# Mixture-of-experts blocks of 32 rows on four column tiles, in place of 64 rows on two

## The chip, the cores and the metric

The kernel runs on one core of a Trainium2 chip. The metric is the device time of one execution in microseconds. All matrix products here are in float32; a 512-column product is recorded as two passes of TensorE, each with its own weight load.

## The reference

Two layers work on 256 context and 1024 latent tokens of width 1024. Layer 0 mixes tokens by attention and a two-way recurrent scan, layer 1 by differential attention. Behind each stands a mixture of experts: every token picks one of four groups and in it two of eight experts, so 32 experts share 2560 assignments in layer 0 and 2048 in layer 1 (context rows are no longer needed there). An expert computes

```python
def run_block(args):
    xblk, e = args
    return (jax.nn.silu(xblk @ w_gate[e]) * (xblk @ w_up[e])) @ w_down[e]
```

with `w_gate[e]` and `w_up[e]` of 1024 x 512 and `w_down[e]` of 512 x 1024. The assignments are sorted by expert and each expert's segment is padded to whole blocks. The block size doesn't enter the result. Each expert has 6.3 MB of weights, each layer 201 MB.

## The kernel before

The program is a chain of phases with a barrier between them. For the mixture of layer `l` they are: `norm_phase` with the tag `nb` (RMSNorm and modulation, rows `h` to DRAM, their transpose kept in SBUF), `route_phase` (router products, choice of experts, ranks, the slot of each assignment, and a small table for the sequencers), `experts_phase`, and `combine_phase` (gathers two result rows a token, weights and adds them).

`experts_phase` (L2175) takes tiles of 128 rows, each two blocks of `BR = 64` rows; the two blocks of a tile may belong to different experts. Layer 0 has 28 tiles, layer 1 has 27 (56 and 53 blocks of 64, from the routing of the reference's inputs). The five engines each run their own loop over the tiles:

- SyncE fetches weights, expert after expert, into a ring of `WR = 3` slots: gate, up and down are one DMA of 2 MB each (L2221). `fetch` waits until the expert that held the slot has done this part (`g_done`, `u_done`, `y_done`); `arrived` (L2224) then passes on that the expert before has landed (`w_ready`, L2227). The view is `"e (k p) n -> p e k n"`: partition p holds rows p, p + 128, ... of the matrix, in pieces of 2 KB for gate and up and 4 KB for down.
- GpSimd gathers the 128 rows of the next tile by token number, 4 KB a row (L2276).
- TensorE multiplies. `products` (L2301) runs one product for the two blocks side by side: output partitions 0 to 63 are block 0 (L2306, weight slot through a register), partitions 64 to 127 block 1 (L2309, slot chosen by three `pe.If`, one for each slot). The order in a tile is gate, up, transposes of the next tile's rows (L2291), transposes of the hidden values (L2321), down in two halves. Every tile reads a code from the table and takes the slots and the number of experts needed from it (L2297 to L2299).
- ScalarE copies the transposed rows, applies SiLU to the gate bank, copies half of the result and issues its store to `yb` (L2354).
- VectorE multiplies SiLU(gate) by up (L2367), copies the transposed hidden values (L2369) and the other half of the result (L2373).

In layer 0 SyncE also writes zeros to the tiles of `yb` that no block fills (L2245). Within `route_phase` VectorE works out the table (L2135 to L2170) while GpSimd scatters the token numbers to their slots.

Of the kernel before, what the change touches and what calls it, by code (L numbers as in the profile page):

```python
# [21 lines left out]
P = 128  # L22
# [20 lines left out]
MODS = 6 * D  # L43
SHIFT1, SCALE1, GATE1, SHIFT2, SCALE2, GATE2 = range(6)
# [115 lines left out]
def norm_phase(nc, sems, tag, d, layer, which, src, hT, ident_dram, rows_out=None, first=0):  # L160
# [5 lines left out]
    with ExitStack() as ctx:  # L166
# [19 lines left out]
        lead_done = s.sem("lead_done")  # L186

# [13 lines left out]
        with nc.Block() as block:  # L201
# [61 lines left out]
            def _(dve):  # L263
# [7 lines left out]
                def body(j, n, par, cond):  # L271
                    for u in range(2):
# [12 lines left out]
                        nc.vector.tensor_tensor(h[:, u, :], h0[:, u, :], mod[:, cond, 0, :], ALU.add).then_inc(h_done, 1)  # L285
# [8 lines left out]
            @block.tensor  # L294
            def _(pe):
                pe.sem_inc(tr_free, 4)
                pe.wait_ge(const_in, 16 * 5)

                def body(j, n, par, cond):
                    for u in range(2):  # L300
                        pe.wait_ge(h_done, 2 * n + u + 1)
                        for b in range(2):

                            pe.wait_ge(tr_free, 4 * n + 2 * u + b + 1)
                            for k in range(4):
                                kk = 4 * b + k
                                last = nc.tensor.transpose(tr[u][b][:, k * P:(k + 1) * P], h[:, u, kk * P:(kk + 1) * P], ident[:, :])
                            last.then_inc(tr_done, 1)
                pairs(pe, body)
# [1626 lines left out]
BR = 64  # L1936
NPM = (2 * TOK + NE * (BR - 1)) // BR // 2 + 1
NPT = NPM + 1
NBT = 2 * NPT
WR = 3  # L1940
CAP = TOK // BR


T_NP, T_EXP, T_PEND, T_CODE = 0, 1, 1 + NE, 1 + 2 * NE
T_COLS = T_CODE + NPT

# [13 lines left out]
def route_phase(nc, sems, tag, d, layer, hT, first, slot_dram, slots, gates, tok, table):  # L1960
# [3 lines left out]
    with ExitStack() as ctx:  # L1964
# [21 lines left out]
        cmp = s.sb("cmp", [P, NBT * NE])  # L1986
        sf = s.sb("sf", [P, 2, T])
        tf = s.sb("tf", [P, T_COLS])
        bo = s.sb("bo", [P, 2, NBT])
        back = s.sb("back", [NPT, P])  # L1990
# [7 lines left out]
        NC_IN = 16 * 8  # L1998

        with nc.Block() as block:  # L2000
            @block.sync
            def _(sp):
                wv = lambda w: w.rearrange("(k p) n -> p k n", p=P)
# [9 lines left out]
                sp.dma_start(desc[:, :], d["desc"]).then_inc(c_in, 16)  # L2013

                sp.wait_ge(zeroed, 1)
                sp.dma_start(slot_dram.rearrange("(n p) o -> n (p o)", p=P), zero[0:NPT, :]).then_inc(filled, 16)
                sp.wait_ge(scattered, 16 * 2 * T)
                sp.dma_start(back[:, :], slot_dram.rearrange("(n p) o -> n (p o)", p=P)).then_inc(back_in, 16)
# [14 lines left out]
            def _(pe):  # L2033
# [15 lines left out]
                pe.wait_ge(back_in, 16)  # L2049
                nc.tensor.transpose(bankT[:, 0:NPT], back[:, :], ident[0:NPT, 0:NPT]).then_inc(back_t, 1)  # L2050

# [11 lines left out]
            def _(dve):  # L2063
# [71 lines left out]
                c.did(V.tensor_scalar(steps[:, 0:2 * NPT], iota[:, 0:2 * NPT], float(BR), None, ALU.mult))  # L2135
# [18 lines left out]

                c.did(V.tensor_scalar(steps[:, 0:NPM], iota[:, 0:NPM], 2.0, None, ALU.mult))
                tally(tf[:, T_PEND:T_PEND + NE], rows_(col(BO), NE, NPM), cols_(steps[:, 0:NPM], NE, NPM), ALU.is_gt, NE, NPM)
                c.did(V.tensor_copy(tf[:, T_NP:T_NP + 1], tf[:, T_PEND + NE - 1:T_PEND + NE]))
# [4 lines left out]
                c.did(V.tensor_scalar(steps[:, 0:NE // WR + 1], iota[:, 1:NE // WR + 2], float(WR), None, ALU.mult))  # L2162
                q = NE // WR + 1
                tally(bo[:, 1, :], rows_(bo[:, 0, :], NBT, q), cols_(steps[:, 0:q], NBT, q), ALU.is_ge, NBT, q)
                c.did(V.scalar_tensor_tensor(out=bo[:, 1, :], in0=bo[:, 1, :], scalar=-float(WR), in1=bo[:, 0, :], op0=ALU.mult, op1=ALU.add))
                code = tf[:, T_CODE:T_CODE + NPT]
                c.did(V.tensor_scalar(code, bo[:, 0, 1:NBT:2], float(WR * WR), float(WR * WR), ALU.mult, ALU.add))
                c.did(V.scalar_tensor_tensor(out=code, in0=bo[:, 1, 0:NBT:2], scalar=float(WR), in1=code, op0=ALU.mult, op1=ALU.add))
                c.did(V.tensor_tensor(code, bo[:, 1, 1:NBT:2], code, ALU.add))
                c.did(V.tensor_copy(table[:, :], tf[0:1, :]))  # L2170
                dve.wait_ge(back_t, 1)
                c.did(V.tensor_copy(tok[:, :], bankT[:, 0:NPT]))


def experts_phase(nc, sems, tag, d, layer, rows, yb, tok, table, fill):  # L2175
# [7 lines left out]
    HT = EH // P  # L2183
    with ExitStack() as ctx:
# [3 lines left out]
        idx = s.sb("idx", [P, 1], U32)  # L2188
        x = s.sb("x", [P, D])
        xT = s.sb("xT", [P, KT, P])  # L2190
        sg, a = s.sb("sg", [P, EH]), s.sb("a", [P, EH])
        aT = s.sb("aT", [P, HT, P])
        y = s.sb("y", [P, D])
        tr = [s.ps(f"tr{b}") for b in range(2)]
        bG, bU, bA = s.ps("bG"), s.ps("bU"), s.ps("bA")
        bY = [s.ps(f"bY{b}") for b in range(2)]
        c_in, idx_done, x_in, xtr, xT_done = (s.sem(n) for n in (
            "c_in", "idx_done", "x_in", "xtr", "xT_done"))
        w_in = [[s.sem(f"w_in{part}{u}") for u in range(WR)] for part in ("gate", "up", "down")]
        w_ready = [s.sem(f"w_ready_{part}") for part in ("gate", "up", "down")]  # L2200
        g_done, u_done, sg_done, a_done, atr, aT_done, y_done, ye_act, ye_dve, y_out = (s.sem(n) for n in (
            "g_done", "u_done", "sg_done", "a_done", "atr", "aT_done", "y_done", "ye_act", "ye_dve", "y_out"))
        go, ended, filled, zeroed = (s.sem(n) for n in ("go", "ended", "filled", "zeroed"))
        zero = s.sb("zero", [P, D])
        wv = lambda name: d[name][layer].rearrange("e (k p) n -> p e k n", p=P)

        def load(eng, col, most, least=0):
            return eng.value_load(table[0:1, col], min_val=least, max_val=most)

        with nc.Block() as block:  # L2210
            @block.sync
            def _(sp):
                sp.dma_start(ident[:, :], d["ident"]).then_inc(c_in, 16)

                def fetch(u, e, tiles, part):

                    if tiles is not None:

                        sp.wait_ge((g_done, u_done, y_done)[part], (1, 1, 2)[part] * tiles)
                    name, at, kk, n = (("moe_w_gate", 0, KT, EH), ("moe_w_up", UP, KT, EH), ("moe_w_down", DOWN, HT, D))[part]  # L2220
                    sp.dma_start(w[:, u * WCOLS + at:u * WCOLS + at + kk * n].rearrange("p (o k n) -> p o k n", o=1, n=n),  # L2221
                                 wv(name)[:, ds(e, 1), :, :]).then_inc(w_in[part][u], 16)
# [6 lines left out]
                def step(o, u, free, before):  # L2229

                    e = load(sp, ds(o + T_EXP, 1), NE - 1)
                    tiles = load(sp, ds(o + (T_PEND - WR), 1), NPM, 1) if free else None
# [7 lines left out]
                if fill:  # L2240

                    sp.wait_ge(zeroed, 1)
                    n = load(sp, slice(T_NP, T_NP + 1), NPM)
                    with sp.Fori(n, NPT) as i:
                        sp.dma_start(yb[ds(i * P, P), :], zero[:, :]).then_inc(filled, 16)  # L2245
# [8 lines left out]
                if fill:  # L2254
# [3 lines left out]
                    sp.wait_ge(filled, 16 * NPT)  # L2258
                    sp.sem_inc(ended, 1)

            @block.gpsimd
            def _(pool):
                nc.gpsimd.memset(zero[:, :], 0.0).then_inc(zeroed, 1)
                n = load(pool, slice(T_NP, T_NP + 1), NPM)
                nc.gpsimd.tensor_copy(idx[:, :], tok[:, 0:1]).then_inc(idx_done, 1)
                pool.wait_ge(idx_done, 1)
                nc.gpsimd.indirect_dma_start(x[:, :], None, rows[:, :], bass.IndirectOffsetOnAxis(idx[:, 0:1], 0)).then_inc(x_in, 16)
                with pool.Fori(0, n) as i:

                    pool.wait_ge(x_in, 16 * i + 16)  # L2270
                    nc.gpsimd.tensor_copy(idx[:, :], tok[:, ds(i + 1, 1)]).then_inc(idx_done, 1)
                    pool.wait_ge(idx_done, i + 2)
                    pool.wait_ge(xtr, 2 * i + 2)

                    pool.sem_inc(go, 1)
                    nc.gpsimd.indirect_dma_start(x[:, :], None, rows[:, :], bass.IndirectOffsetOnAxis(idx[:, 0:1], 0)).then_inc(x_in, 16)  # L2276
# [352 lines left out]
```

## Time and profile before

| | us |
|---|---|
| median of 3 runs | 5791.07 |
| lowest, highest | 5783.55, 5791.42 |
| the profiled execution | 5788.05 |
| its span | 5785.7 |

The profile is one execution taken by the hardware profiler. The span runs from its first to its last instruction. "PE" is TensorE's matmuls, "PEld" its weight loads, which overlap them, "PEldq" its sequencer's own work (loads of registers, arithmetic, branches), which isn't counted as busy. PEclk is the granted clock of TensorE as a share of 2.4 GHz. "DMA share" is the mean busy share of the 16 DMA engines; overlapping packets let it pass 1.

### The profile page before, as it was taken

What the parts mean: (1) busy time and instruction counts of PE and PEld (TensorE: products, weight loads), DVE (VectorE), ACT (ScalarE), POOL (GpSimd) and SP (SyncE); (2) the same over time, 40 slices, a digit from 0 to 9 for tenths busy, and PEclk for the clock granted to TensorE, in tenths of its full rate; (3) what the DMA queues carried; (4) which work ended last, traced back from release to release, by engine and by line L of the source; (5) the groups of instructions that cost most, each with busy time, mean ns of one, the idle gap of its engine ahead of it and who ended that gap; (6) DMA issues with size and microseconds to landing.
All of it is one profiled execution on the core that took longest, in us unless ns stands there. A gap on an engine that the chain in (4) does not pass through costs nothing. (4 is left out here: it accounts for less than half of the span.)

```text
span 5785.7 us, 71070 instructions
## 1 busy us (share of the span) xinstructions
PE 4182.2 (72%) x23474; PEld 2739.1 (47%) x23475; DVE 2196.7 (38%) x4254; ACT 1422.0 (25%) x3188; POOL 639.3 (11%) x1135
## 2 busy tenths in 40 slices
PE   5597599395876949574499983598199955497893
PEld 1385377284765838453133321487056644132331
DVE  0312544666556656624000002411677733200003
ACT  0210254343333424212011110210056622011111
POOL 0000000131322313300100002000300010100001
PEclk9798799697988969786799996799599977799997
DMA  9421100101010010133886697322510023799943
GB/s 336 147 86 68 62 9 9 38 1 25 10 25 10 0 34 1 46 128 109 312 339 235 228 377 282 118 89 76 193 49 10 11 98 105 274 364 397 374 165 145
DMA packets 350063, 778.83 MB, mean 135 GB/s; under 512 B 52000, under 2 KB 95284, under 8 KB 349796
## 3 DMA queue, kind: packets, MB, share of 16 engines
q1 hardware_dynamic: 297640, 624.64, 30.1%
q10 hardware_dynamic: 37696, 103.04, 4.6%
q0 software_dynamic: 14544, 48.79, 2.4%
q8 instruction: 105, 1.72, 0.1%
q14 instruction: 78, 0.64, 0.0%
HBM read 656.45 MB, written 122.58 MB: 135 GB/s over the span
## 5 line engine op out<-in xcount | busy, mean ns | idle before, releaser
L2306 PE MATMUL ex_bG<-ex_w,ex_xT 128*64 x880 | 424.7, 639 | 134.5 <-SPq L2227 77.3
L2306 PE MATMUL ex_bY<-ex_w,ex_aT 128*64 x880 | 392.6, 599 | 74.5 <-DVE ex_aT L2369 59.7
L2309 PE MATMUL ex_bG<-ex_w,ex_xT 128*64 128x512 f32 x880 | 424.7, 639 | 0.0
L367 PE MATMUL p_acc<-hT,p_wh 128*128 128x512 f32 (+1 forms) x1056 | 376.2, 356 | 24.6 <-DVE p_wl L379 24.6
L2309 PE MATMUL ex_bY<-ex_w,ex_aT 128*64 128x512 f32 x880 | 392.8, 600 | 0.0
L2306 PE MATMUL ex_bU<-ex_w,ex_xT 128*64 x880 | 386.6, 592 | 0.0
L2309 PE MATMUL ex_bU<-ex_w,ex_xT 128*64 128x512 f32 x880 | 386.6, 592 | 0.0
L2367 DVE TENSOR_TENSOR ex_a<-ex_sg,ex_bU 128x512 f32<-128x512 f32 x55 | 37.9, 688 | 917.9 <-PE ex_bU L2309 917.9
L367 PE MATMUL p_acc<-hT_rest,p_wh 128*128 128x512 f32 (+1 forms) x1056 | 375.7, 356 | 0.0
L367 PE MATMUL p_acc<-hT,p_wl 128*128 128x512 f32 (+1 forms) x1056 | 375.2, 355 | 0.0
L2306 PEld LDWEIGHTS ex_bG<-ex_w,ex_xT 128*64 128x64 f32 x880 | 127.9, 148 | 415.3 <-issue 415.3
L703 PE MATMUL ad_S<-ad_K,ad_q 64*128 64x512 f32 (+1 forms) x768 | 193.5, 584 | 125.2 <-DMA ad_lqk<-in_od_lk 120.8
L2306 PEld LDWEIGHTS ex_bY<-ex_w,ex_aT 128*64 128x64 f32 x880 | 116.7, 138 | 306.5 <-issue 306.5
L777 DVE TENSOR_SCALAR_CACHE_REDUCE ad_p<-ad_S 128x512 f32<-128x512 f32 (+1 forms) x384 | 215.7, 600 | 100.5 <-PE ad_S L703 100.5
L2306 PEld LDWEIGHTS ex_bU<-ex_w,ex_xT 128*64 128x64 f32 x880 | 120.6, 137 | 248.7 <-issue 248.7
L388 DVE COPY p_o<-p_acc 128x512 f32<-128x512 f32 x88 | 49.1, 558 | 469.5 <-PE p_acc L367 468.7
L367 PEld LDWEIGHTS p_acc<-hT,p_wh 128*128 128x128 f32 x1056 | 200.9, 190 | 53.9 <-issue 25.4
L1354 PE MATMUL rs_bankZ<-rs_X,rs_Bm 128*128 128x128 f32 x1280 | 224.7, 277 | 0.0
L1351 PE MATMUL rs_bankY<-rs_ident,rs_X 128*128 128x128 f32 x640 | 185.1, 289 | 47.3 <-DVE rs_Bm L1558 39.0
L367 PEld LDWEIGHTS p_acc<-hT_rest,p_wh 128*128 128x128 f32 x1056 | 201.0, 190 | 27.9
L367 PEld LDWEIGHTS p_acc<-hT,p_wl 128*128 128x128 f32 x1056 | 200.6, 190 | 28.2
L1450 ACT ACTIVATE rs_Y<-rs_bankY 128x256 f32<-128x256 f32 x320 | 122.4, 384 | 350.3 <-PE rs_bankZ L1354 350.2
(362 smaller groups left out, 8841.4 us busy)
## 6 DMA issues: line engine op xcount, KB each, us to landing
ex_w<-in_moe_w_gate SPq DMA_DIRECT2D x64, 2048.0 KB, 17.8
ex_w<-in_moe_w_up SPq DMA_DIRECT2D x64, 2048.0 KB, 21.2
ex_w<-in_moe_w_down SPq DMA_DIRECT2D x64, 2048.0 KB, 18.1
mods_w<-in_mod_w SPq DMA_DIRECT2D x24, 2048.0 KB, 13.0
projT_dram<-p_o ACTq DMA_DIRECT2D x44, 640.0 KB, 2.9
yb_dram<-ex_y ACTq DMA_DIRECT2D x55, 512.0 KB, 6.3
p_w<-in_od_w_in SPq DMA_DIRECT2D x12, 1024.0 KB, 5.1
n_x<-x_dram SPq DMA_DIRECT2D x20, 512.0 KB, 4.1
```

Source lines behind the costliest of these rows:

```text
L367: mm = nc.tensor.matmul(acc[u % 2][c][:, 0:n], a[:, u // 2, k, at], b[:, k, t0:t0 + n], start=k == 0 and x == 0, stop=k == KT - 1 and x == 2)
L388: nc.vector.tensor_copy(o[:, u % 2, t0:t0 + n], acc[u % 2][c][:, 0:n]).then_inc(dve_ev, 1)
L703: x = nc.tensor.matmul(S[j % 2][c][:, 0:w], q[h, pair, t * P - q_from:(t + 1) * P - q_from], K[h, kmap(pair), a:a + w], start=True, stop=True)
L777: nc.vector.tensor_scalar(p[:, u, c, a:a + w], S[j % 2][c][:, 0:w], 1.0, None, ALU.mult, ALU.max, accum_out=top[:, u, c, i:i + 1]).then_in ...
L1351: nc.tensor.transpose(bankY[g][:, dr * P:(dr + 1) * P], X[:, g, dr, :], ident[:, :])
L1354: x = nc.tensor.matmul(to, Bm[:, g, dr, l, :], X[:, g, dr, :], start=True, stop=True)
L1450: aa.did(f"X{g}" if l == 1 else f"Y{l}{g}", nc.scalar.activation(to[:, g, :, :], bankY[g][:, 0:256].rearrange("p (d t) -> p d t", d=2), AC ...
L2306: nc.tensor.matmul(bank[0:BR, :], stationary[:, k, 0:BR], w[:, ds(slot0 + (offset + k * n), 512)], start=k == 0, stop=k == tiles - 1)
L2309: m = nc.tensor.matmul(bank[BR:P, :], stationary[:, k, BR:P], w[:, at:at + 512], start=k == 0, stop=k == tiles - 1)
L2367: nc.vector.tensor_tensor(a[:, :], sg[:, :], bU[:, :], ALU.mult).then_inc(a_done, 1)
```

## The change

- **Blocks.** `BR` is 32. A block is the unit of every loop. There are 97 in layer 0 and 83 in layer 1 (from the same routing); before, with the padding, there were 28 x 4 = 112 and 27 x 4 = 108 such units of 32 rows.
- **Four column tiles.** One matmul call fills 32 output partitions and takes 256 columns of weights. In `hidden` the four groups are the left and right half of gate and the left and right half of up, into one bank `bH`: partitions 0 to 63 gate, 64 to 127 up. In `down` the four groups are the quarters of the 1024 output columns, in one bank `bY`.
- **Rows as quarters.** `h` in DRAM is cut into four pieces of 256 values a row; one gather fetches 32 rows x 4 pieces of 1 KB to 128 partitions. The token list is spread to quarters in `route_phase`.
- **Neighbouring weight rows on a partition.** The gate and up views are `(p k)`: partition p holds rows 8p to 8p + 7, 16 KB in one piece. Down is `(g p h)` with h = 2: pieces of 8 KB. To match, the norm phase writes `h` in another order of columns (`placed`), its transposes read with a step of 2, and so do the transposes of the experts phase.
- **Order on TensorE.** A block's `down` is put behind the next block's `hidden`. Tiles x, xT, sg, a, aT, y and all PSUM banks are doubled.
- **Evictions.** ScalarE keeps SiLU and the stores, VectorE makes all PSUM copies.
- Each block reads the table twice (`place`), once for `hidden` and once for `down`, and each has a chain of three `pe.If`.

```diff
-BR = 64
+BR = 32
+CAP = TOK // BR
+NBM = (2 * TOK + NE * (BR - 1)) // BR
+NBT = NBM + 3
 WR = 3
...
-                        nc.vector.tensor_tensor(h[:, u, :], h0[:, u, :], mod[:, cond, 0, :], ALU.add).then_inc(h_done, 1)
+                        nc.vector.tensor_tensor(placed(h[:, u, :]), natural(h0[:, u, :]), natural(mod[:, cond, 0, :]), ALU.add).then_inc(h_done, 1)
...
-                        sp.wait_ge((g_done, u_done, y_done)[part], (1, 1, 2)[part] * tiles)
+                        sp.wait_ge((h_done, h_done, y_done)[part], tiles)
...
+                    if part < 2:
+                        sp.dma_start(to.rearrange("p (o k n) -> p o k n", o=1, n=n),
+                                     d[name][layer].rearrange("e (p k) n -> p e k n", k=kk)[:, ds(e, 1), :, :]).then_inc(w_in[part][u], 16)
+                    else:
+                        sp.dma_start(to.rearrange("p (o g n) -> p o g n", o=1, g=2),
+                                     d[name][layer].rearrange("e (g p h) n -> p e g (h n)", g=2, h=2)[:, ds(e, 1), :, :]).then_inc(w_in[part][u], 16)
...
+                def turn_rows(p, landed, b=None):
+                    pe.wait_ge(x_in[p], 16 * landed)
+                    if b is not None:
+                        pe.wait_ge(a_done, b + 1)
+                    for e in range(2):
+                        t = nc.tensor.transpose(bX[p][:, e * P:(e + 1) * P], x[:, p, e:XC:2], ident[:, :])
+                    t.then_inc(xtr, 1)
+                def place(b):
+                    code = load(pe, ds(b + T_CODE, 1), WR * (NE + 1) - 1, WR)
+                    return code // WR, code % WR
+                def hidden(p, u):
+                    for c in range(XG):
+                        for e in range(2):
+                            for g in range(4):
+                                at = u * WCOLS + (0, UP)[g // 2] + (2 * c + e) * EH + g % 2 * HC
+                                m = nc.tensor.matmul(bH[p][g * BR:(g + 1) * BR, 0:HC], xT[:, p, e, c, :], w[:, at:at + HC],
+                                                     start=c == 0 and e == 0, stop=c == XG - 1 and e == 1)
+                    m.then_inc(h_done, 1)
+                def down(p, u):
+                    for k in range(HT):
+                        for g in range(4):
+                            at = u * WCOLS + DOWN + k * D + g * XC
+                            m = nc.tensor.matmul(bY[p][g * BR:(g + 1) * BR, 0:XC], aT[:, p, k % 2, k // 2, :], w[:, at:at + XC], start=k == 0, stop=k == HT - 1)
+                    m.then_inc(y_done, 1)
+                def turn_hidden(p):
+                    for h in range(2):
+                        t = nc.tensor.transpose(bA[p][:, h * 2 * BR:(h + 1) * 2 * BR], a[2 * BR:P, p, h:HC:2], ident[2 * BR:P, 2 * BR:P])
+                    t.then_inc(atr, 1)
+                def block_down(b, p):
+                    need, slot = place(b)
+                    pe.wait_ge(w_ready[2], need)
+                    pe.wait_ge(aT_done, b + 1)
+                    for u in range(WR):
+                        with pe.If(slot == u):
+                            down(p, u)
...
                 with pe.Fori(0, n) as i:
+                    for q in PAR:
+                        b, p = 2 * i + q + 1, 1 - q
+                        need, slot = place(b)
+                        for part in range(2):
+                            pe.wait_ge(w_ready[part], need)
+                        pe.wait_ge(xT_done, b + 1)
                         for u in range(WR):
+                            with pe.If(slot == u):
+                                hidden(p, u)
+                        block_down(b - 1, 1 - p)
+                        turn_rows(p, i + q + 2, b)
+                        turn_hidden(p)
```

## Rows read from the trace of the kernel before

**Rows 1.** The page's first part: busy time, share of the span, instructions.

```profile
PE 4182.2 (72%) x23474; PEld 2739.1 (47%) x23475; DVE 2196.7 (38%) x4254; ACT 1422.0 (25%) x3188; POOL 639.3 (11%) x1135
```

**Rows 2.** Windows over both expert phases: stretch, length, busy us, PEclk, DMA share, GB/s.

```profile
2777.00:3537.00 760.00, 649.68 (x3024) 235.91 (x3026) 57.29 (x83) 100.95 (x142) 33.32 (x59) 0.94 0.83 310
4960.00:5700.00 740.00, 624.71 (x2924) 228.59 (x2924) 55.26 (x80) 97.40 (x137) 31.94 (x55) 0.94 0.83 310
```

**Rows 3.** Timeline of TensorE in one tile: start, us, engine, line, operation, [idle before].

```profile
5443.11 0.59 PE L2306 MATMUL ex_bU<-ex_w,ex_xT 128*64 x1
...
5449.55 0.59 PE L2306 MATMUL ex_bU<-ex_w,ex_xT 128*64 x1
...
5450.08 1.10 PE L2291 MATMUL ex_tr<-ex_ident,ex_x 128*128 128x128 f32 x8
5451.02 0.65 PE L2321 MATMUL ex_bA<-ex_ident,ex_a 128*128 128x128 f32 x4
5453.03 0.64 PE L2306 MATMUL ex_bY<-ex_w,ex_aT 128*64 x1 [1.36 <-DVE ex_aT L2369]
...
5466.81 0.59 PE L2306 MATMUL ex_bU<-ex_w,ex_xT 128*64 x1
```

**Rows 4.** Waits of TensorE in the two expert phases: total us, times, longest.

```profile
PE ex_bG L2306 <- SPq L2227: 27.1, 4, 8.4
PE ex_bY L2306 <- DVE ex_aT L2369: 24.5, 20, 1.7
...
PE ex_bG L2306 <- SPq L2227: 50.3, 6, 19.6
```

**Rows 5.** Windows: experts bound by weights; 2 KB pieces of mod_w; 5 KB pieces.

```profile
5300.00:5420.00 120.00, 89.76 (x390) 31.06 (x392) 6.96 (x11) 12.68 (x18) 4.23 (x8) 0.87 1.04 397
60.00:140.00 80.00, 57.32 (x222) 10.30 (x218) 8.77 (x13) 0.00 (x0) 0.00 (x0) 0.85 0.95 356
4190.00:4200.00 10.00, 8.94 (x24) 3.45 (x24) 6.19 (x24) 3.00 (x5) 0.00 (x0) 0.50 1.03 419
```

**Rows 6.** TensorE's sequencer by line: count, ns min/median/max, first and last start.

```profile
L2304 PEldq COMPARE_BRANCH  x660: 68/200/379, 2788.5 to 5695.9; - x165
...
L2208 PEldq TENSOR_LOAD <-table x57: 297/304/492, 2778.0 to 5673.0; - x57
L2208 PEldq FUSED_REGOPS  x57: 151/157/165, 2778.5 to 5673.3; - x57
...
L2295 PEldq FUSED_REGOPS  x55: 59/59/64, 2785.8 to 5672.9; - x55
```

**Rows 7.** Sequencer's branches at 5443.2 to 5449.9; then matmuls of ex_bU after.

```profile
L2304 PEldq COMPARE_BRANCH  x1: 200/200/200, 5445.7 to 5445.7; - x1
...
5445.75:5450.00 4.25, 4.25 (x22) 1.28 (x18) 0.00 (x0) 1.00 1.02 396
```

**Rows 8.** Sequencer before and in the first product of ex_bY; then ten small transposes.

```profile
L2304 PEldq COMPARE_BRANCH  x2: 68/138/207, 5452.4 to 5452.7; - x2
...
L2306 PEldq FUSED_REGOPS  x4: 46/46/150, 5452.8 to 5453.3; - x4
...
2713.83 0.78 PE L2042 MATMUL rt_bankL<-rt_ident,rt_lgT 36*128 36x36 f32 x10 [0.56 <-ACT rt_lgT L2056]
```

**Rows 9.** Evictions of PSUM (page, timeline), and landing of the row gathers.

```profile
L2367 DVE TENSOR_TENSOR ex_a<-ex_sg,ex_bU 128x512 f32<-128x512 f32 x55 | 37.9, 688 | 917.9 <-PE ex_bU L2309 917.9
...
2713.31 0.38 ACT L2056 ACTIVATE rt_lgT<-rt_acc 36x256 f32<-36x256 f32 x1 [2.86 <-PE rt_acc L2037]
...
DMA to landing us min/median/max: 4.0/7.5/9.0
```

**Rows 10.** VectorE's timeline: norm rows, a stepped read in routing, tok.

```profile
2662.25 1.23 DVE L285 TENSOR_TENSOR nb_h<-nb_h,nb_mod 128x1024 f32<-128x1024 f32 x1 [0.24 <-DMA h_dram<-nb_h]
...
2718.02 0.72 DVE L2093 TENSOR_REDUCE rt_w<-rt_big 128x80 f32<-128x320 f32 x1
...
2774.89 0.20 DVE L2172 CAST tok<-rt_bankT 128x37 uint32<-128x37 f32 x1 [18.12 <-PE rt_bankT L2050]
```

More of the change, by code:

```diff
@@ L2182, in experts_phase @@
     UP, DOWN = KT * EH, 2 * KT * EH
-    HT = EH // P
+    HT, HC = EH // P, EH // 2
+    PAR = range(2)
     with ExitStack() as ctx:
@@ L2263, in _, with gather @@
                 nc.gpsimd.memset(zero[:, :], 0.0).then_inc(zeroed, 1)
[L2264 to L2267, printed above, removed]
-                with pool.Fori(0, n) as i:
[L2270 to L2276, printed above, removed]
+                n = half(pool)
+                def gather(b, p):
+                    nc.gpsimd.tensor_copy(idx[:, p:p + 1], tok[:, ds(b, 1)]).then_inc(idx_done, 1)
+                    pool.wait_ge(idx_done, b + 1)
+                    pool.sem_inc(go, 1)
+                    nc.gpsimd.indirect_dma_start(x[:, p, :], None, pieces, bass.IndirectOffsetOnAxis(idx[:, p:p + 1], 0)).then_inc(x_in[p], 16)
+                gather(0, 0)
+                gather(1, 1)
+                pool.wait_ge(xtr, 1)
+                gather(2, 0)
+                with pool.Fori(0, n) as i:
+                    for u in PAR:
+                        pool.wait_ge(xtr, 2 * i + u + 2)
+                        gather(2 * i + u + 3, 1 - u)
             @block.tensor
@@ L2280, in _ @@
                 pe.wait_ge(c_in, 16)
-                n = load(pe, slice(T_NP, T_NP + 1), NPM)
-                def turn(i, again):
-                    pe.wait_ge(x_in, 16 * i + 16)
-                    for b in range(2):
-                        if again:
-                            pe.wait_ge(xT_done, 2 * i - 1 + b)
-                        for k in range(4):
-                            t = nc.tensor.transpose(tr[b][:, k * P:(k + 1) * P], x[:, (4 * b + k) * P:(4 * b + k + 1) * P], ident[:, :])
-                        t.then_inc(xtr, 1)
@@ L2356, in _, with gated, store @@
-                act.wait_ge(y_out, 16 * n + 16)
+                n = half(act)
+                def gated(b, p):
+                    act.wait_ge(h_done, b + 1)
+                    nc.scalar.activation(sg[2 * BR:P, p, :], bH[p][0:2 * BR, 0:HC], ACT.Silu).then_inc(sg_done, 1)
+                def store(b, p):
+                    act.wait_ge(ye_done, b + 1)
+                    act.dma_start(yb[ds(b * BR, BR), :].rearrange("t (c n) -> c t n", c=XG), y[:, p, :]).then_inc(y_out[p], 16)
+                for u in PAR:
+                    act.sem_inc(y_out[u], 16)
@@ L2485, in _ @@
                     act.wait_ge(x_out[u], 16 * rounds)
-CONSTS = ("cos", "sin", "ident", "ones", "blockones", "headones", "headcols", "tri", "first", "levels", "before", "iota", "tokid", "desc")
+CONSTS = ("cos", "sin", "ident", "ones", "blockones", "headones", "headcols", "tri", "first", "levels", "before", "iota", "tokid", "desc", "quad")
 def build(nc, d, out):
```

213 lines of the change are left out of this document (106 added, 107 removed).

## The prediction

> **What bounds the kernel now.** I read the page first. TensorE is busy for 4182 of 5786 us, more than any other engine [rows 1]. The change touches the two expert phases, so I cut windows over them: 760 us and 740 us, together 1500 us, with TensorE busy for some 85% and the DMA engines for 83% [rows 2]. Neither is full over the phase, so the limit must change from tile to tile. The timeline of a tile gives the first side. In the product of up, 15 passes lie between 5443.11 and 5449.55, 0.429 us each; a pass is 512 columns on both column tiles at once. From one tile's up to the next tile's it is 23.7 us [rows 3] (23.5 below, as most tiles are a little shorter). The other side is the weights. Where each block brings a new expert, the DMA engines are at 1.04 with 397 GB/s [rows 5]. At that rate an expert's 6.29 MB take 15.8 us and each tile's 1.05 MB of rows and results 2.6 us more: 34.2 us for a tile with two new experts, 18.4 with one. TensorE's waits for weights stand in the list of waits, 27 and 50 us, on ten tiles [rows 4].
>
> Both together explain the phases. Layer 0 has 9 tiles of 28 with two new experts, layer 1 has 11 of 27 (from the routing of the reference's inputs). The sum over tiles of the larger side is 19 x 23.5 + 9 x 34.2 = 754 us and 16 x 23.5 + 11 x 34.2 = 752 us: 1506 against 1500 measured. I use the same rule for the changed kernel and take the 6 us off again.
>
> **Array time of a block.** A pass of `hidden` or `down` has 256 columns, so 0.214 us if its four groups run side by side as the two do now. `hidden` has 8 steps of two passes, 3.42 us; `down` has 4, 1.71 us. Twelve transposes took 0.94 us for the first eight, 0.117 each, and 0.10 us passes between the last product and the first of them [rows 3]. Four transposes with two such changes are 0.67 us. The array needs 5.8 us a block. Four blocks make 23.2 us for 128 rows, the same as a tile today; what is saved is padding, 180 blocks in place of 220 units of 32 rows (97 and 83 against 112 and 108). With 5.8 us a block nothing would be lost.
>
> **What the sequencer needs.** Here I find the cost. Today a tile reads the table once and runs 12 tests of an If (660 for 55 tiles); the load takes 0.30 us, the operation behind it 0.16, the address 0.06, a taken branch 0.20 and one not taken 0.07 [rows 6]. Between two such instructions about 0.06 us passes: the first test starts at 5452.4, the second at 5452.7, the registers at 5452.8, the first matmul at 5453.03 [rows 3, 8]. A read of the table with what follows (some three more operations of 0.05 and seven gaps) is then 1.1 us; a chain of three tests is 0.26 + 0.26 + 0.13 = 0.65 us, part of it ahead of the body and part behind.
>
> Today this is hidden by a queue. The last branch of the up product starts at 5445.7, with all its matmuls issued, and 22 matmuls run in the 4.25 us after it, two of which had begun: 20 are queued, ten passes of two [rows 7]. With four matmuls in a pass of 0.214 us the same 20 last for five passes, 1.07 us. The changed block has two reads of the table and two chains. From the last matmul of `hidden` to the first of `down` the sequencer needs 0.65 + 1.1 + 0.1 for a second wait = 1.85 us, 0.8 more than the queue holds; a restart costs 0.05 (0.64 us for the first pass's matmul, 0.59 for others [rows 3]): 0.85 us idle. From the last matmul of `down` it needs the rest of the chain (0.26), two waits (0.2), half a loop end (0.15), the table (1.1), three waits (0.3) and the next chain's head (0.39): 2.4 us, against 1.07 of queue and 0.67 of transposes: 0.7 us idle. The block comes to 5.8 + 0.85 + 0.7 = 7.4 us. The ends: 5.8 if the queue hides all, 8.2 if nothing of `down` is queued when its waits come. I take 7.4, since the rows price each part.
>
> Other waits of a block stay inside these. `down` of block b-1 needs aT, copied during `hidden` of block b. The transposes of b wait for its product: SiLU on 256 columns (0.38 us) and a VectorE product of half of today's 0.69 us, with a drain of 0.2 behind `hidden`, some 1.2 us [rows 9], under idle and `down` (2.6). Gathers land in 7.5 us, at most 9.0, plus 2 us on GpSimd, and have two blocks, 14.8 us. VectorE's four copies are 1.6 us a block. These cost nothing; at 5.8 us a block the gather (11 of 11.6 us) would be late next.
>
> **Weights.** Pieces of 16 KB and 8 KB replace 2 KB and 4 KB. At full DMA share, 2 KB pieces give 356 / 0.95 = 375 GB/s and 5 KB pieces 419 / 1.03 = 407 [rows 5]. On 16 engines that is 87 ns and 201 ns a piece: 13 ns fixed and 37 ns per KB. At 16 KB this gives 433 GB/s, at 8 KB 424, so 14.6 us an expert in place of 15.8. No row shows such pieces; the bounds are 14.6 and 15.8 (no gain), above it if long pieces hold up the short ones. I take 14.6, as both rows lie on the straight line. Rows and results are 0.74 us a block (1 KB pieces by the same line, 128 each way).
>
> **The sum.** An expert of n blocks costs the larger of 7.4 n and 14.6 + 0.74 n. With one or two blocks it is the weights (15.3 and 16.1), from three on TensorE. Layer 0 has 7 experts with one block, 12 with two, and 66 blocks in the rest: 107 + 193 + 488 = 788 us. Layer 1 has 17, 5 and 56 blocks: 260 + 81 + 414 = 755 us. Together 1543, less the same 6, is 1537: 37 us more than now. The expert with 18 blocks alone costs 133 us, today 106.
>
> Small parts: the stepped write of 18 norm tiles, between 0 and 1 us each (today 1.23 us for 1024 elements; a stepped read took 0.72 for 320 [rows 10]), on a path with other waits: 3 us. The table of VectorE grows by 3 us, but VectorE idles for 18 us ahead of `tok` [rows 10]: 0. Two more operations behind it and the wait for up before the first product: 2 us. Total +42: the profiled execution at 5788.05 becomes 5830; the median of the runs shown is 3 us above it (5791), so 5833.
>
> The Trainium skill, TensorE: Matmul & The Clock Gate, the table at its head, gives TensorE a queue of 64 instructions. By this rule 32 loads and 32 matmuls would be queued, 1.7 us; the rows show 20 matmuls [rows 7], and the measurement decides. What the rule would make of the time is the first rival.
>
> **Rivals.** First, the sequencer stays hidden, because the queue holds more or the tests and reads cost less than I add up. It decides below 7.1 us a block, where the sum (768 + 738 - 6) equals today's 1500. For it: today no idle stands between tiles. Against: the count of 20, and 0.64 us from test to matmul. With 6.1 us a block the sum is 703 + 683 - 6 = 1380, so -120 + 5: 5676. Chance 0.25. By the skill's 64 entries the gaps shrink to about 0.2 and 0.1 us, 6.1 us a block.
>
> Second, the pieces gain nothing: 15.8 us an expert, so 812 + 782 - 6 = 1588, +88 + 5: 5884. For it, 1.04 share at 397 GB/s may be a limit of the memory; against, the 419. Chance 0.12.
>
> Third, matmuls don't go side by side four at a time or are issued too slowly. At half the overlap a block is over 11 us, and the time above 6200. For it: ten small transposes came 0.062 us apart, four would be 0.25 a pass; against, four register operations with 16 matmuls behind them issue in 0.6 us [rows 8]. Chance 0.06. The same page, "Wait — 56ns, not 53.3ns?", gives 62 ns a matmul when the sequencer decodes in software; by it a pass is 0.25 us and a block over 9 us, some 300 us more. The trace agrees with the figure in the transposes and not in the product.
>
> **How the numbers follow.** My forecast has 0.50 (7.1 to 7.9 us a block, 5796 to 5894), something between it and the first rival 0.07. Slower by over 0.2% (what a measurement can tell): 0.43 of the forecast, 0.12 and 0.06 make 0.61. Faster: 0.25, 0.05 and 0.02 make 0.32. Within: 0.07. The range reaches from 5670, just below the first rival, to 5940, 8.0 us a block with weights between their bounds.
>
> **What would show it.** Right: ex_bH passes every 0.21 us with four matmuls; idle put down to issue ahead of ex_bY and ex_bH of 0.85 and 0.7 us; 7.4 us from block to block within the 18-block expert; over 420 GB/s at full share; ACT_TABLE_LOAD gone without effect. Wrong: blocks under 7 us, passes over 0.25 us, waits for x or w_ready inside large experts.

## The result, and the profile after

| | before | changed |
|---|---|---|
| median | 5787.31 us | 5931.49 us |
| lowest, highest of 4 | 5781.98, 5791.42 | 5928.19, 5947.03 |
| the profiled execution, its span | 5788.05, 5785.7 | 5947.03, 5945.2 |

The changed kernel is slower by the ratio 1.0256, 95% interval 1.0243 to 1.0268: +144 us. The forecast was 5833, +42. The direction was right, the size a third of what came.

The page's first part of the changed kernel answers to [rows 1]: half again as many matmuls, no more TensorE time.

```profile
PE 4154.5 (70%) x35526; PEld 2968.8 (50%) x35527; DVE 2348.9 (40%) x4815; ACT 1292.6 (22%) x3091; POOL 786.9 (13%) x1389
```

Windows over the two expert phases, from the first fetch of weights to the issue of the last store; they answer to [rows 2]. The columns are stretch, length, busy us of PE, PEld, DVE, ACT, POOL, then PEclk, DMA share, GB/s.

```profile
2788.70:3642.00 853.30, 662.43 (x9704) 366.99 (x9704) 140.71 (x390) 37.12 (x98) 114.17 (x197) 0.90 0.67 269
5068.60:5863.20 794.60, 586.17 (x8304) 323.97 (x8304) 120.14 (x334) 31.64 (x84) 97.94 (x169) 0.86 0.70 281
```

Counted in the same way the kernel before took 762.6 and 741.1 us. The phases grew by 90.7 and 53.5 us, 144 of the 159.5 us between the two profiled spans; this execution was the slowest of the four. (Norm and routing grew by 4.9 and 2.5 us; the rest lies outside these phases.) DMA share fell from 0.83 to 0.67 and 0.70 and TensorE was hardly busier, so something new is waited for. The list of waits, whole span, names it (total us, times, longest):

```profile
DVE ex_y L2424 <- DMA yb_dram<-ex_y: 553.7, 61, 13.8
...
PE ex_bY L2339 <- DVE ex_aT L2419: 214.7, 49, 8.8
...
PE ex_bH L2331 <- SPq L2252: 80.8, 10, 13.7
```

VectorE, about to copy a result into `y`, waits for the store that used this buffer two blocks ago. Behind that copy in its queue stand the copy of the transposed hidden values and the next rows, and TensorE's `down` waits for them. One such place, from the timeline of all engines while weights arrive:

```profile
3022.93 0.42 DVE L2424 COPY ex_y<-ex_bY 128x256 f32<-128x256 f32 x1 [1.26 <-PE ex_bY L2339]
3023.52 0.55 ACTq L2390 DMA_DIRECT2D yb_dram<-ex_y  x1
...
3030.72 0.56 ACTq L2390 DMA_DIRECT2D yb_dram<-ex_y  x1
...
3037.56 3.66 PE L2331 MATMUL ex_bH<-ex_w,ex_xT 128*32 128x256 f32 x64 [0.21 <-issue]
...
3041.05 0.42 DVE L2424 COPY ex_y<-ex_bY 128x256 f32<-128x256 f32 x1 [5.77 <-DMA yb_dram<-ex_y]
3041.39 0.28 DVE L2419 COPY ex_aT<-ex_bA 128x128 f32<-128x128 f32 x1
3041.59 0.41 DVE L2411 COPY ex_xT<-ex_bX 128x256 f32<-128x256 f32 x1
```

The two buffers of `y` take turns, so the copy at 3041.05 fills the buffer of the copy at 3022.93, whose store was issued at 3023.52. By the DMA packets of the trace (128 of 1 KB to a store, counted in order) the last packet of that store ends at 3040.4: 16.9 us for 128 KB. The next store, issued at 3030.72, takes 11.2 us. Of the 180 stores 86 take over 10 us, the longest 32. The reason shows where a store runs with no other DMA beside it (a window of 0.8 us, then the same in the first experiment's kernel, whose only edit is the store's shape):

```profile
3060.10:3060.90 0.80, 0.80 (x20) 0.52 (x16) 0.00 (x0) 0.00 (x0) 0.08 (x1) 1.00 0.27 93
```

```profile
3067.90:3068.30 0.40, 0.40 (x16) 0.25 (x12) 0.00 (x0) 0.00 (x0) 0.35 (x1) 1.00 0.86 305
```

Share 0.27 at 93 GB/s is four DMA engines of 16 at work; 0.86 at 305 GB/s is nearly all of them. The packets agree: mostly four are in flight at a time in the first window, up to 16 in the second. The store of the changed kernel is written `"t (c n) -> c t n"`: its outermost dimension is 4. The Trainium skill, DMA: Bandwidth & Descriptors, section "Why a DMA increments its semaphore by 16 and not by 1", says that a DMA is spread over the largest number up to 16 that divides the outermost dimension of both sides; the trace agrees (0.27 against 0.25).

What was forecast of the weights came true. Five blocks that each bring a new expert answer to the first of [rows 5], 397 GB/s:

```profile
5464.00:5546.00 82.00, 41.59 (x500) 21.95 (x500) 7.84 (x23) 1.88 (x5) 5.77 (x10) 0.71 1.01 426
```

And so did the layout of a block on TensorE, but for its size. The timeline of two blocks in the expert with 18 answers to [rows 3]:

```profile
5765.82 3.66 PE L2331 MATMUL ex_bH<-ex_w,ex_xT 128*32 128x256 f32 x64 [0.20 <-issue]
5769.78 1.94 PE L2339 MATMUL ex_bY<-ex_w,ex_aT 128*32 128x256 f32 x32 [0.29 <-issue]
5771.64 0.51 PE L2318 MATMUL ex_bX<-ex_ident,ex_x 128*128 128x128 f32 x2
5772.08 0.45 PE L2345 MATMUL ex_bA<-ex_ident,ex_a 64*128 64x64 f32 x2
5772.46 3.66 PE L2331 MATMUL ex_bH<-ex_w,ex_xT 128*32 128x256 f32 x64
5776.28 1.93 PE L2339 MATMUL ex_bY<-ex_w,ex_aT 128*32 128x256 f32 x32 [0.16 <-issue]
...
5779.24 3.66 PE L2331 MATMUL ex_bH<-ex_w,ex_xT 128*32 128x256 f32 x64 [0.22 <-issue]
```

6.64 and 6.78 us from block to block, idle of at most 0.29 us ahead of a product, where 7.4 with 0.85 and 0.7 was forecast. ACT_TABLE_LOAD, 55 times in the two phases before, runs once in each now, as forecast.

### The profile page after: what moved, and what is told of

It is laid out like the page before. It is cut to its first block and busy times, and to the rows that moved or that the text cites. A ratio compares the mean times of both kernels' runs of the same rounds, so it can differ in the third digit from the quotient of the medians.

```text
span 5945.2 us, 98711 instructions
## 1 busy us (share of the span) xinstructions
PE 4154.5 (70%) x35526; PEld 2968.8 (50%) x35527; DVE 2348.9 (40%) x4815; ACT 1292.6 (22%) x3091; POOL 786.9 (13%) x1389
## 5 line engine op out<-in xcount | busy, mean ns | idle before, releaser
L2331 PE MATMUL ex_bH<-ex_w,ex_xT 128*32 128x256 f32 x11520 | 693.6, 395 | 115.9 <-SPq L2252 80.8
L2339 PE MATMUL ex_bY<-ex_w,ex_aT 128*32 128x256 f32 x5760 | 408.8, 429 | 260.3 <-DVE ex_aT L2419 214.7
L2331 PEld LDWEIGHTS ex_bH<-ex_w,ex_xT 128*32 128x32 f32 x11520 | 376.1, 114 | 365.7 <-issue 162.3
L2339 PEld LDWEIGHTS ex_bY<-ex_w,ex_aT 128*32 128x32 f32 x5760 | 200.8, 121 | 453.9 <-issue 386.6
L2386 ACT ACTIVATE ex_sg<-ex_bH 64x256 f32<-64x256 f32 x180 | 67.5, 375 | 1567.1 <-PE ex_bH L2331 1044.4
L2424 DVE COPY ex_y<-ex_bY 128x256 f32<-128x256 f32 x180 | 76.3, 424 | 749.8 <-DMA yb_dram<-ex_y 553.7
L2415 DVE TENSOR_TENSOR ex_a<-ex_sg,ex_bH 64x256 f32<-64x256 f32 x180 | 76.4, 425 | 573.2 <-ACT ex_sg L2386 573.2
L1364 PEld LDWEIGHTS rs_bankZ<-rs_X,rs_Bm 128*128 128x128 f32 x1280 | 205.7, 201 | 0.0
L1550 DVE TENSOR_TENSOR rs_X<-rs_X,rs_bankY 128x256 f32<-128x256 f32 x320 | 134.2, 421 | 180.7 <-PE rs_bankY L1374 176.8
L736 PE MATMUL ad_acc<-V,ad_pT 128*128 128x128 f32 x1280 | 187.7, 286 | 17.9 <-ACT ad_pT L858 17.9
```

The costliest lines, as they stand in the source:

```text
L736: x = nc.tensor.matmul(acc[m % 2][:, c * HD:c * HD + VW], pT[:, g % 3, k * P:(k + 1) * P], V[:, kt, vc:vc + VW], start=kt == 0, stop=kt == ...
L1364: x = nc.tensor.matmul(to, Bm[:, g, dr, l, :], X[:, g, dr, :], start=True, stop=True)
L1550: va.did(f"X{l}{g}", nc.vector.tensor_tensor(X[:, g, :, :], X[:, g, :, :], corr, ALU.subtract))
L2331: m = nc.tensor.matmul(bH[p][g * BR:(g + 1) * BR, 0:HC], xT[:, p, e, c, :], w[:, at:at + HC], start=c == 0 and e == 0, stop=c == XG - 1 an ...
L2339: m = nc.tensor.matmul(bY[p][g * BR:(g + 1) * BR, 0:XC], aT[:, p, k % 2, k // 2, :], w[:, at:at + XC], start=k == 0, stop=k == HT - 1)
L2386: nc.scalar.activation(sg[2 * BR:P, p, :], bH[p][0:2 * BR, 0:HC], ACT.Silu).then_inc(sg_done, 1)
```

## The experiments

All are compared with the kernel before in the same series; medians, ratio with 95% interval. "Phases" is the sum of both expert phases, or L0 and L1 by layer, from the first fetch to the last store: 762.6 and 741.1 before, 853.3 and 794.6 changed. The expectations count up to the last store but one, which is some 7 us less for every kernel with blocks of 32. Where a kernel's values are not the reference's, layer 1 routes its tokens a little otherwise (81 blocks in place of 83, or 26 tiles in place of 27, in two of them), so between such kernels L0 is the sound comparison.

### The store as one run: what four engines cost

```diff
-act.dma_start(yb[ds(b * BR, BR), :].rearrange("t (c n) -> c t n", c=XG), y[:, p, :])
+act.dma_start(yb[ds(b * BR, BR), :].rearrange("t (c n) -> (t c) n", c=XG), y[:, p, :])
```

> The changed kernel with one edit: a block's result is stored to one run of 128 KB, 128 pieces of 1 KB counted by partition, where it was four strides of 32 rows. The same bytes and pieces; the quarters land at wrong places in yb, so the values are not the reference's. Theory A (the store's outer dimension of 4 puts it on 4 of the 16 DMA engines, 32 pieces each behind weight pieces of 0.61 us, about 20 us where a block takes 7): the wait of VectorE's result copies for the store (553.7 us in 61 waits) falls under 50 us, blocks are paced by 6.8 us or by 15.3 us of weights an expert, the expert phases take 1471 us by that sum where the changed kernel took 1644, and the time falls by 120 to 180 us, to about 5780. Theory B (the store is late because its pieces queue behind 16 KB pieces on whichever engine): the wait stays above 400 us, the time within 40 us of 5931. Theory C (the wait only covers another limit, TensorE's sequencer or the weights): the wait goes, the time falls by less than 40 us.

Measured: 5735.37 us, ratio 0.9920 (0.9904 to 0.9937): 196 us less than the changed kernel, and faster than before. Phases 742.9 and 694.3, DMA share and rate up again:

```profile
2775.40:3518.30 742.90, 639.05 (x9704) 364.00 (x9704) 143.71 (x390) 37.26 (x98) 114.62 (x197) 0.95 0.75 309
4955.00:5649.30 694.30, 562.29 (x8304) 319.40 (x8304) 123.06 (x334) 31.59 (x84) 98.32 (x169) 0.91 0.78 322
```

No wait for a store is left in the list; VectorE's copy now waits for TensorE:

```profile
DVE ex_y L2424 <- PE ex_bY L2339: 268.4, 180, 8.3
```

By the packets no store takes over 9.8 us now. Theory A holds, with more than it promised. One dimension of one access pattern was worth more than the whole change.

### The zero blocks as one run

```diff
-sp.dma_start(yb[ds(i * BR, BR), :].rearrange("t (c n) -> c t n", c=XG), zero[:, :])
+sp.dma_start(yb[ds(i * BR, BR), :].rearrange("t (c n) -> (t c) n", c=XG), zero[:, :])
```

> The changed kernel with one edit: the zero blocks of layer 0 are written as one run of 128 KB each by partition, in place of four strides. Only the 12 and more writes behind the third expert's weights change. Theory A: the 25 us in which SyncE issues them fall under 8 us, the gaps of 19 to 22 us between blocks 2 to 4 shrink, and the time falls by 10 to 25 us. Theory B: SyncE's issues wait for the weights ahead of them in its queue, whatever their shape: under 5 us.

Measured: 5924.35 us, ratio 1.0243 (1.0220 to 1.0266), which the interval doesn't part from the changed kernel. L0 is 844.2 against 853.3, 9 us less, but L1, which this edit doesn't touch, is 7 us shorter too (787.6), so the difference is within what two executions differ by. SyncE's 17 issues span 18 us in place of 33, where theory A wanted under 8. By itself this run decides nothing. Two kernels below that have this edit, with their stores mended, take 729.5 and 733.3 us in L0 against 742.9 without it, and no less in L1: there it is worth some 10 us.

### Pieces of 2 and 4 KB again, with either store

```diff
-d[name][layer].rearrange("e (p k) n -> p e k n", k=kk)
+d[name][layer].rearrange("e (k p) n -> p e k n", k=kk)
...
-d[name][layer].rearrange("e (g p h) n -> p e g (h n)", g=2, h=2)
+d[name][layer].rearrange("e (g p) n -> p e g n", g=4)
```

> The changed kernel with the weights fetched as before the change, rows p, p + 128, ... on a partition in pieces of 2 KB (gate, up) and 4 KB (down); stores still in four strides. The rows meet the wrong weights, so the values are not the reference's. Theory A (four engines, each piece of the store waits for one piece of weights ahead of it): with pieces of 84 ns in place of 611 ns the store's 32 turns take about 32 x (0.05 + 0.1) = 5 us in place of 20, the wait of VectorE for the store falls from 553.7 us to under 200, but an expert's weights take 16.0 + 0.74 us; the sum for 6.8 us a block is 1528 us, so the time falls by 60 to 120 us, to 5810 to 5870. Theory B (long pieces are not the reason, only the number of engines): the wait stays over 400 us and the time rises by 10 to 50 us, to 5940 to 5980.

> Both edits: the store as one run by partition, the weights in pieces of 2 and 4 KB; values not the reference's. It measures against the kernel with the store alone what the long pieces are worth once stores are on time. By the sums for 6.8 us a block: 1528 against 1471 us, so 57 us slower than the kernel with the store edit alone (about 5840). If long pieces hold up stores and gathers on any engine, it is the faster of the two.

Measured: 5878.91 us with the strided store, ratio 1.0166 (1.0149 to 1.0183), and 5779.08 with the store as one run, 0.9993 (0.9984 to 1.0003). With the strided store short weight pieces are 53 us *better* (theory A promised 60 to 120), with the other 44 us *worse* (57 expected). So the long pieces are good by themselves and made the four-engine store worse. By the packets the slowest store takes 32 us beside long pieces and 11 us beside short ones, which fits theory A, that on each engine 32 pieces of 1 KB take turns with pieces of weights. With short pieces no wait for a store shows at all, and yet the strides still cost 53.8 us in L0 (807.2 against 753.4), where the waits for weights tell why. First the strided store, then the other (whole span):

```profile
PE ex_bH L2331 <- SPq L2252: 204.2, 26, 14.5
```

```profile
PE ex_bH L2331 <- SPq L2252: 140.0, 19, 12.6
```

If four engines also carry all the results, they bring their share of an expert later than the other twelve. The packets bear this out. While weights are among them, only three to six packets are in flight at once for 48 us of L0 with the strided store and for 3 us with the other; in the changed kernel and with the store as one run it is 44 and 4 us. The trace has no number of the engine of a packet, so that these are the four engines of the stores is inferred.

### Does the order on VectorE matter?

```diff
                         product(b, p)
-                        result(b - 1, 1 - p, i)
                         hidden_turned(b, p)
                         rows_turned(b + 2, p)
+                        result(b - 1, 1 - p, i)
```

> The changed kernel, stores in four strides, with VectorE's copy of a result (which waits for the store of two blocks before) moved behind its copies of the transposed hidden values and of the next rows, so that a late store doesn't hold up the down product of its own block. Theory A1 (the order is what turns a late store into lost time): the time falls by 100 us or more. Theory A2 (with two result tiles and a store that takes 10 to 20 us while weights stream, the pace is the store's, wherever VectorE waits): it falls by less than 50 us; the wait on the store stays above 350 us.

Measured: 5946.23 us, ratio 1.0287 (1.0269 to 1.0305), phases 854.8 and 794.3: nothing gained. The wait for the store is 401.6 us in 59 places. Theory A2: where VectorE stands while it waits for the store is no matter.

### Stores in four strides that nobody waits for

```diff
-act.dma_start(yb[ds(b * BR, BR), :].rearrange("t (c n) -> c t n", c=XG), y[:, p, :])
+act.dma_start(yb[ds(b * BR, BR), :].rearrange("t (c n) -> c t n", c=XG), zero[:, :])
...
+                act.wait_ge(zeroed, 1)
...
-                    dve.wait_ge(y_out[p], 16 * i + 16)
```

> The changed kernel with its stores in four strides, but sent from the tile of zeros in place of the result tiles, so that VectorE never waits for a store to land; the results themselves are not stored. The same number, shape and bytes of stores as in the changed kernel. It parts the two things that the four strides may do: land late (VectorE waits), and load 4 of the 16 DMA engines more than the others (weights arrive later). With pieces of 2 KB, where no wait for a store showed, the strides cost 89 us in the expert phases (1562.8 against 1473.7), and with 16 KB pieces 211 us (1640.5 against 1429.8). Theory D (both, and they add): the wait was worth 211 - 89 = 122 us, so the expert phases take 1519 us and the time is 5810. Theory L (late landing is all): 5735, as with the store as one run. Theory U (the uneven load is all, VectorE's wait only covers it): 5931.

Measured: 5856.84 us, ratio 1.0121 (1.0100 to 1.0143), L0 801.0. Of the 110.4 us that the strides cost in L0, 52.3 go with VectorE's wait and 58.1 stay. Neither L nor U; D has the direction, but my reading of what stays was too simple. ScalarE's timeline in a run of small experts shows the wait at another place, and so does the list of waits:

```profile
5223.69 12.20 ACTq L2390 DMA_DIRECT2D yb_dram<-ex_zero  x1
5237.70 9.55 ACTq L2390 DMA_DIRECT2D yb_dram<-ex_zero  x1
5248.82 11.11 ACTq L2390 DMA_DIRECT2D yb_dram<-ex_zero  x1
5261.74 13.24 ACTq L2390 DMA_DIRECT2D yb_dram<-ex_zero  x1
```

```profile
ACT ex_sg L2386 <- issue: 439.8, 32, 25.6
```

An issue otherwise takes 0.56 us; 46 of the 180 took over 1 us, 428 us together. The stores pile up until the issuing engine itself is held, and the next SiLU stands behind it. If more result buffers did what the missing wait does, they would recover half at most; that is an estimate, no run has them. The few packets in flight beside weights are there as before (41 us of L0), but how the rest divides between held issues and late weights stays open.

### Two ways to keep the values and use all engines

Four DMAs of 32 rows, one a quarter; and the quarters side by side on 32 partitions with one store. Both also write the zero blocks as one run.

```diff
+for c in range(XG):
+    act.dma_start(yb[ds(b * BR, BR), c * XC:(c + 1) * XC], y[c * BR:(c + 1) * BR, p, :]).then_inc(y_out[p], 16)
...
```

```diff
-y = s.sb("y", [P, 2, XC])
+y = s.sb("y", [BR, 2, D])
...
+for c in range(XG):
+    m = nc.vector.tensor_copy(y[:, p, c * XC:(c + 1) * XC], bY[p][c * BR:(c + 1) * BR, 0:XC])
...
+act.dma_start(yb[ds(b * BR, BR), :], y[:, p, :]).then_inc(y_out[p], 16)
```

> The changed kernel with each quarter of a result stored by its own DMA, 32 partitions with 1 KB each, four from ScalarE a block, the reference's values; the zero blocks written as one run. Theory A (what matters is how many of the 16 DMA engines a store is spread over): each of the four has 32 rows as outer dimension, so 2 pieces an engine; the expert phases take what they took with the store as one run (1430 us) less the 16 us of the zero blocks: about 5720 us, 5700 to 5745; the 4 x 0.34 = 1.4 us of issue a block lie in ScalarE's 6 us of idle time. Theory B (ScalarE's issues hold up the next SiLU, 1.0 us a block on the path of 122 blocks where TensorE is the bound): 5840.

> The changed kernel with VectorE copying the four quarters of a result side by side onto 32 partitions (four copies of 32 x 256 in place of one of 128 x 256), and one store of 32 rows of 4 KB; the reference's values; the zero blocks written as one run. Theory A: 2 pieces of 4 KB an engine; VectorE works about 3 x 0.41 = 1.2 us more a block, ahead of the copy of the transposed hidden values, which in blocks of 6.6 us is ready 3.4 us before TensorE needs it: about 5715 us, within 15 us of the kernel with four stores. Theory B (VectorE comes onto the path): 0.5 to 1.2 us in each of 122 blocks, 5780 to 5860.

Measured: 5728.14 us, ratio 0.9903 (0.9887 to 0.9920), and 5723.87 us, ratio 0.9899 (0.9883 to 0.9916). Theory A in both: 1.4 us more of issue on ScalarE and some 1.2 us more of copies on VectorE a block cost nothing that these times show. These two also show that the gain doesn't hang on the misplaced quarters of the store as one run.

### One read of the table more, and half a read less

The first edit is to the kernel with the store as one run, the second to the one with results on 32 partitions. In the second, `held` is the slot that the block's `hidden` has read.

```diff
                         b, p = 2 * i + q + 1, 1 - q
+                        load(pe, ds(b + T_CODE, 1), WR * (NE + 1) - 1, WR)
                         need, slot = place(b)
```

> The kernel with the store as one run by partition (5735.4 us; values not the reference's) with one more read of the table by TensorE's sequencer ahead of each hidden product, about 1.1 us. In the prediction half of such a read was put on TensorE's path. Theory P (reads and branches are partly on the path): 0.5 to 1.1 us in each of the 122 blocks of experts that TensorE bounds: +60 to +130 us, 5795 to 5865. Theory H (the sequencer works while the matmuls queued before it run, as 6.6 to 7.0 us a block suggest): under +15 us.

```diff
-                        block_down(b - 1, 1 - p)
+                        block_down(b - 1, 1 - p, held if q else None)
+                        held = need, slot
...
```

> The kernel with results side by side on 32 partitions (5723.9 us) where every second down product takes the slot that the hidden product of the same block has read, in place of reading the table again: one of four reads fewer in two blocks; the reference's values. One more read a block cost 67 us; half a read fewer would give back 67 / 2 = 33 us if TensorE still waits for its sequencer in the mended kernel as much as it did with the read added (5690); 10 to 25 us if only part of the blocks wait; nothing (within 8 us) if the sequencer is hidden without the added read.

Measured: one more read a block gives 5802.48 us against 5735.37, +67 us, phases 782.6 and 720.3 (+39.7 and +26.0). Within short blocks (under 8.2 us from product to product in the timeline) the mean goes from 6.8 to 7.35 us, half of the 1.1 us that I priced a read at. Theory P. Half a read less gives 5714.50 us, ratio 0.9885 (0.9869 to 0.9902), 9.4 us less than 5723.87. The two intervals overlap, and 9.4 us lies between nothing (8) and the weak form (10 to 25). The traces say more: the mean of the short blocks goes from 6.83 to 6.72 us, a fifth of the 0.55 us that half a read was priced at, in 150 blocks, and the phases (723.9 and 692.1) are 16.8 us shorter. That is the weak form: in the mended kernel part of the reads is still in sight, most of it is hidden. This is the fastest version found, 67 us below the kernel before in the same series (5781.18).

### The long pieces in the kernel before

```diff
-wv = lambda name: d[name][layer].rearrange("e (k p) n -> p e k n", p=P)
+wv = lambda name: d[name][layer].rearrange("e (p k) n -> p e k n", p=P)
```

> The kernel before, blocks of 64 rows on two column tiles, with one edit: gate, up and down fetched with neighbouring rows on a partition, one piece of 16 KB each, in place of pieces of 2 and 4 KB; rows meet the wrong weights, so the values are not the reference's. Theory G (the two halves of the change are worth little without each other: 64-row tiles keep TensorE the bound at 23.4 us wherever a tile needs one new expert): only the 20 tiles that need two new experts gain, 2 x 1.4 us each: -55 us by that sum, to about 5730. Theory S (long pieces also delay the stores and gathers that the tile waits for): within 15 us of 5787. If -55 comes, long pieces alone in the kernel before are worth what the changed kernel gains once its stores are mended (5724 to 5728).

and the same with stepped transposes, so that every row meets its weights:

```diff
-t = nc.tensor.transpose(tr[b][:, k * P:(k + 1) * P], x[:, (4 * b + k) * P:(4 * b + k + 1) * P], ident[:, :])
+t = nc.tensor.transpose(tr[b][:, k * P:(k + 1) * P], x[:, 4 * b + k:D:KT], ident[:, :])
...
-t = nc.tensor.transpose(bA[:, k * P:(k + 1) * P], a[:, k * P:(k + 1) * P], ident[:, :])
+t = nc.tensor.transpose(bA[:, k * P:(k + 1) * P], a[:, k:EH:HT], ident[:, :])
```

> The kernel before with weights in pieces of 16 KB (5729.05 us, values wrong there) made right in the smallest way: TensorE's transposes read the rows with a step of 8 columns and the hidden values with a step of 4, so that tile k meets weight rows 8p + k and 4p + k; norm, routing and gathers stay as they were. Theory P (a stepped read by the transposes costs nothing): 5729, within 10 us. Theory Q (a step of 8 floats slows the twelve transposes of a tile, from 0.12 to 0.25 us each): 1.5 us in each of the 35 tiles that TensorE bounds, +50 us, 5780.

Measured: 5729.05 us, ratio 0.9906 (0.9890 to 0.9923), and 5738.71 us, ratio 0.9928 (0.9909 to 0.9947). The first hit its expectation to a microsecond, but for a partly wrong reason: its layer 1 ran 26 tiles, since its routing differs. In L0 both take 745.8 and 745.9 us; the stepped one takes 720.3 in L1 where the other took 705.0. So the stepped reads cost nothing in L0, and the pieces are worth 16.7 + 20.8 = 37.5 us in the phases, not the 55 that the sum gives. (The rows of these transposes: first before, then stepped.)

```profile
L2291 PEld LDWEIGHTS ex_tr<-ex_ident,ex_x x456: 137/141/231, 2785.7 to 5691.1; 128*128 128x128 f32 x152
L2291 PE MATMUL ex_tr<-ex_ident,ex_x x456: 272/273/476, 2785.7 to 5691.2; 128*128 128x128 f32 x152
```

```profile
L2291 PEld LDWEIGHTS ex_tr<-ex_ident,ex_x x456: 185/193/231, 2780.4 to 5642.4; 128*128 128x128 f32 x152
L2291 PE MATMUL ex_tr<-ex_ident,ex_x x456: 274/276/480, 2780.4 to 5642.5; 128*128 128x128 f32 x152
```

Three short edits to the kernel before bring 44 us in its median (5782.7 in that series). Blocks of 32 rows on four column tiles, with stores mended, end 15 us lower (5723.87 against 5738.71), and 24 with the read saved.

## Why the prediction went wrong, step by step

- **What bounds the kernel.** Right: per expert the larger of TensorE's and the weights' time, nothing else in the phases before.
- **Rows and results, "0.74 us a block (1 KB pieces by the same line, 128 each way)", and "these cost nothing".** This step failed. It spread the store over all 16 engines, and in the list of waits that stay inside a block the store's own landing, for which VectorE waits with TensorE behind it, is missing. The kernel before stores 128 rows and no wait for it shows; I carried that over without looking at the new pattern's outermost dimension, 4. The store as one run brings the phases from 1648 to 1437 us: the step was worth 211 us and priced at nothing. The rule that gives it stands in the section of the Trainium skill named above and would have been a rival to weigh. What is shown: that the shape is the cause, that the number of engines is what the shape changes, that long weight pieces aggravate it, that VectorE's order doesn't cure it and that taking its wait away cures half (52 of 110 us in L0).
- **A block of 7.4 us.** Too large; it is 6.8 (the mean is 6.84 us over the changed kernel's 120 blocks under 8.2 us). The array part was too small, about 6.4 in place of 5.8: `hidden` 3.66 against 3.42, `down` 1.94 against 1.71, transposes 0.96 against 0.67. The idle part was too large, about 0.4 in place of 1.55. A read of the table is only half in sight when added; of half a read taken away, a fifth comes back. With 6.8 in the sum the phases fall by 72 us, from 1537 to 1465.
- **Weights, 14.6 us an expert.** The rate was right: 426 GB/s at 1.01 share, where 424 to 433 were worked out for long pieces. The rival that they gain nothing is out. In total they were worth less than the sum says: 44 us in the phases with the store as one run (1481 against 1437), where the sum gives 57, and 37.5 of 55 in the kernel before. The sum itself runs high: the phases with the store as one run are 28 us under 1465. That fetches run two experts ahead and so hide a part would explain both, but no run shows it.
- **Together:** 1537 - 72 - 28 + 211 = 1648, as measured. The oversized block and a sum that runs high hid 100 of the 211 us in the forecast. That the slower direction came true is luck: without the store's landing the same kernel is faster. So is it that 5931 lies under the 5940 at which the range ends, for that end stands for blocks of 8.0 us, which didn't come.
- **The rival of a hidden sequencer** (6.1 us a block, 5676) decides at 7.1 us, and its side is the true one: 6.8. With its stores mended the kernel is faster, 5724, by 60 us where this rival said 115. **Four tiles not side by side** is out: a pass of four takes 3.66 / 16 = 0.23 us, 0.057 us a matmul.
- **Small parts:** norm and routing 7.4 us against 5.

## What to carry to other kernels

For each DMA in a change, read the outermost dimension of its pattern on both sides as closely as its bytes and pieces: a factor of 4 there put a transfer on four engines. With hardly another DMA beside it, it took 3.0 us from issue to its last packet; beside weights it took 16.9 us in the place shown, and up to 32. Ask for every buffer that is now filled and emptied twice as often who waits for it to be empty, and what stands behind that wait. And split a change into its parts before crediting it: here the view of the weights alone, three edits in the old kernel, gave 44 of the 67 us that the best version has.

## What the runs showed of the hardware

- A store of 128 pieces in four strides takes 0.56 us to issue, one over 16 engines 0.34 us (medians of 180), so the shape costs the issuing engine too.

```profile
L2390 ACTq DMA_DIRECT2D yb_dram<-ex_y x180: 554/559/1213, 2820.5 to 5863.2; - x180
```

```profile
L2390 ACTq DMA_DIRECT2D yb_dram<-ex_y x180: 338/343/362, 2810.6 to 5649.3; - x180
```

- From issue to last packet a store on four engines took 3.0 us at the least and 32 at the most, one over 16 engines 1.4 and 9.8 us, with weights in pieces of 16 and 8 KB. With pieces of 2 and 4 KB the most was 11 and 6.1 us.
- Stores that nobody waits for held their issuing engine for up to 22.4 us each.
- Transposes that read every eighth value of a row took 276 ns against 273, their weight loads 193 against 141 ns, hidden beside the matmuls.
